# Second mixer of a three-block network on one Trainium2 core: the attention branch's upward product and half of the output projection in three passes of split halves

## The reference, cut to what matters

```python
m   = sigmoid(g_ssm) * (y_ssm @ w_ssm_up) + sigmoid(g_attn) * (y_attn @ w_attn_up)   # 512 -> 1024
x   = x + m @ w_out                                                                  # 1024 -> 1024
h   = rmsnorm(x, norm2_g)
q   = h @ peer_wq                                                                    # 1024 -> 2048, next stage
```

## Time and profile before

| | before |
|---|---|
| time, median of 3 runs | 2174.49 us (2173.45 to 2175.11) |
| the profiled execution's own time | 2174.43 us |
| its span on the core | 2172.4 us |
| PE, DVE, ACT, POOL busy | 95%, 71%, 52%, 32% of the span |
| mean granted TensorE clock | 0.985 of full speed |
| attn_up's first matmul to the next stage's first matmul | 1280.89 to 1330.44 us |

### The profile page before, as it was taken

The page is one execution under the profiler, slowest core; times in us unless marked ns, Lnnn a source line. Parts: engine busy times, 40 slices in busy tenths (PEclk is TensorE's granted clock), DMA queues, the critical chain, the costliest instruction groups (busy, mean ns, idle before and its releaser), DMA issues. The chain is left out here.

```text
span 2172.4 us, 33584 instructions
## 1 busy us (share of the span) xinstructions
PE 2070.5 (95%) x11152; PEld 1705.5 (79%) x11152; DVE 1543.8 (71%) x2577; ACT 1132.3 (52%) x1648; POOL 698.1 (32%) x478
## 2 busy tenths in 40 slices
PE   4999999998999999999999999999999999999998
PEld 4876767776877776777776656999999998888887
DVE  4377898886467788888878841499587776555555
ACT  5364767774345377777550323355544444454444
POOL 6621030003757414000030004599867662000000
PEclk8999999999999989999999999999999999999999
DMA  9873889994557658999832333355544445555554
GB/s 395 304 289 143 340 329 348 348 350 175 200 213 286 232 220 317 345 351 346 328 103 97 126 117 119 110 187 184 183 141 140 145 143 185 192 188 190 193 191 148
DMA packets 76631, 485.65 MB, mean 224 GB/s; under 512 B 9472, under 2 KB 9984, under 8 KB 58624
## 3 DMA queue, kind: packets, MB, share of 16 engines
q1 hardware_dynamic: 75824, 482.88, 61.6%
q10 hardware_dynamic: 720, 1.61, 0.2%
HBM read 483.41 MB, written 1.05 MB: 223 GB/s over the span
## 5 line engine op out<-in xcount | busy, mean ns | idle before, releaser
L1249 DVE TENSOR_TENSOR moe_w_lo<-ring,moe_w_hi 128x1024 fp32r<-128x1024 f32 x376 | 456.1, 1251 | 43.8 <-ACT moe_w_hi L1167 31.9
L1167 ACT ACTIVATE moe_w_hi<-ring 128x1024 fp32r<-128x1024 f32 x376 | 387.0, 1059 | 87.3 <-PE bank L1100 48.0
L3187 POOL TENSOR_TENSOR peer_u_lo<-peer_u,peer_u_hi 128x512 fp32r<-128x512 f32 x255 | 328.1, 1298 | 91.0 <-ACT peer_u_hi L3213 87.7
L3125 PE MATMUL bank<-peer_hn_hi,peer_u_hi 128*128 128x256 f32 x1024 | 293.2, 286 | 3.7 <-ACTq L3200 3.5
L3126 PE MATMUL bank<-peer_hn_lo,peer_u_hi 128*128 128x256 f32 x1024 | 285.8, 279 | 0.0
L3127 PE MATMUL bank<-peer_hn_hi,peer_u_lo 128*128 128x256 f32 x1024 | 285.6, 279 | 0.0
L1081 PE MATMUL bank<-moe_w_hi,moe_slots_hi 128*128 128x512 f32 x512 | 210.2, 411 | 8.3 <-DVE moe_w_lo L1249 4.1
L3213 ACT ACTIVATE peer_u_hi<-peer_u 128x512 fp32r<-128x512 f32 x253 | 159.0, 629 | 112.8 <-PE bank L3127 111.2
L1083 PE MATMUL bank<-moe_w_hi,moe_slots_lo 128*128 128x512 f32 x512 | 200.9, 392 | 0.0
L1082 PE MATMUL bank<-moe_w_lo,moe_slots_hi 128*128 128x512 f32 x512 | 200.4, 391 | 0.0
L3125 PEld LDWEIGHTS bank<-peer_hn_hi,peer_u_hi 128*128 128x128 f32 x1024 | 192.7, 188 | 4.4 <-issue 3.7
(11 more groups left out here) (526 smaller groups left out, 4556.6 us busy)
## 6 DMA issues: line engine op xcount, KB each, us to landing
ring<-in_stream SPq DMA_DIRECT2D x135, 2048.0 KB, 8.8
peer_u<-in_peer_u SPq DMA_DIRECT2D x128, 512.0 KB, 3.3
peer_scores<-in_peer_v SPq DMA_DIRECT2D x86, 512.0 KB, 4.3
sb_mod_ring<-in_ada_t SPq DMA_DIRECT2D x64, 512.0 KB, 6.7
peer_u<-in_peer_v SPq DMA_DIRECT2D x42, 512.0 KB, 4.3
ret_mod_ring<-in_ada_t SPq DMA_DIRECT2D x32, 512.0 KB, 4.8
s_bz<-in_b_channel SPq DMA_DIRECT2D x4, 512.0 KB, 6.0
ring<-in_stream SPq DMA_DIRECT2D x2, 1024.0 KB, 5.9
```

Of the source, the lines that this page charges most:

```text
L1167: act.activation(w_hi[:, q, :], K.ring[:, at % RING, q * CHUNK // Q:(q + 1) * CHUNK // Q], ACT.Copy).then_inc(hi_done, 1)
L1249: dve.tensor_tensor(w_lo[:, q, :], K.ring[:, at % RING, q * CHUNK // Q:(q + 1) * CHUNK // Q], w_hi[:, q, :].bitcast(F32), ALU.subtract).th ...
L3125: pe.matmul(out, u_hi[:, b, k2, :], h_hi[:, k, :], start=(k == 0), stop=False)
L3187: pool.tensor_tensor(u_lo[:, b, :, :], u[:, i, KD // 2 * half:KD // 2 * (half + 1), :], u_hi[:, b, :, :].bitcast(F32), ALU.subtract).then_ ...
```

## The change

Nothing is changed in what is computed. The upward product of attention and the second half of the projection's columns are made in three passes of halves; they borrow the buffers `w_hi`, `w_lo`, `x_hi`, `x_lo` of the next stage's products.

- GpSimd makes the four low quarters of `attn_up` after its second mask, then those of w_out2's second chunk, then those of `peer_wq`: 12 instead of 4.
- ACT makes the high quarters of `attn_up` in the first four turns of the attention loop, those of the second `w_out2` chunk when `attn_up` is used up, and those of `peer_wq` as `project_split(1)` frees each quarter (`out_used`). It also makes a high half of the turned mix.
- DVE takes each unit's values in two steps, a copy to the high half, a wait for it, and the remainder, and makes the low half of the turned mix (`mixed_low`).
- PE's order of the projection becomes (0,0), turn_mixed(1), (1,0), (0,1), (1,1).
- The squares are taken in the order in which the halves come, and the second tile's last square and square root stand ahead of the last high quarter of `peer_wq`.

```diff
+    SPLIT = (n_attn, n_out + 1)
+    ring_quarter = lambda n, q: K.ring[:, n % RING, q * CHUNK // Q:(q + 1) * CHUNK // Q]
...
+            def split_lows(n):                                       # GpSimd, after the second mask
+                for q in range(Q):
+                    pool.wait_ge(split_high, Q * SPLIT.index(n) + q + 1)
+                    pool.tensor_tensor(w_lo[:, q, :], ring_quarter(n, q), w_hi[:, q, :].bitcast(F32),
+                                       ALU.subtract).then_inc(split_low, 1)
+            for n in SPLIT:
+                split_lows(n)
             queries.low(pool, queries.n0, True)
...
             def attn_up(tt, dh):
-                upward(n_attn, S.yaT, tt, dh, 4 + 2 * tt + dh).then_inc(K.chunk_used if tt and dh else attn_made, 1)
+                out, cols = K.bank[:, 4 + 2 * tt + dh, :], slice(dh * 512, (dh + 1) * 512)
+                for k in range(4):
+                    if tt == 0 and dh == 0:
+                        pe.wait_ge(split_low, k + 1)
+                    high, low = w_hi[:, k, cols], w_lo[:, k, cols]
+                    pe.matmul(out, x_hi[:, k, own(tt)], high, start=(k == 0), stop=False)
+                    pe.matmul(out, x_hi[:, k, own(tt)], low, start=False, stop=False)
+                    last = pe.matmul(out, x_lo[:, k, own(tt)], high, start=False, stop=(k == 3))
+                last.then_inc(K.chunk_used if tt and dh else attn_made, 1)
...
+            def project_split(tt):                                   # takes the place of project_out(tt, 1)
+                n, out = n_out + 1, K.bank[:, 2 * tt + 1, :]
+                for k in range(KD):
+                    q, cols = k // 2, slice(k % 2 * COLS, (k % 2 + 1) * COLS)
+                    if k % 4 == 0:
+                        pe.wait_ge(mix_low, 2 * tt + k // 4 + 1)
+                    if tt == 0 and k % 2 == 0:
+                        pe.wait_ge(split_low, Q + q + 1)
...
+                    if tt == 1 and k % 2 == 1 and k < KD - 1:
+                        last.then_inc(out_used, 1)
...
             turn_mixed(1)
+            project_out(1, 0)
             project_out(0, 1)
-            project_out(1, 0)
             project_out(1, 1)
...
                 take_turned(n)                                       # ScalarE, attention loop
                 if n < TT:
                     take_gate(8 + n, n_last, 3, ACT.Copy)
+                if n < Q:
+                    split_high_quarter(n_attn, n)
...
+                for half in range(2):
+                    act.activation(x_hi[:, 4 * half:4 * half + 4, own(tt)],
+                                   K.bank[:, 4 + 2 * tt + half, :].rearrange("p (k t) -> p k t", k=4), ACT.Copy).then_inc(mix_high, 1)
+                if tt == 0:
+                    act.wait_ge(K.chunk_used, n_attn + 1)
+                    for q in range(Q):
+                        split_high_quarter(n_out + 1, q)
...
-            queries.high(act, queries.n0, True)
-            square(0)
-            square(1)
+            square(0, 0)
+            square(2, 1)
+            square(1, 2)
             deviation(0)
-            square(2)
-            square(3)
-            deviation(1)
+            for q in range(Q):
+                if q == Q - 1:
+                    square(3, 3)
+                    deviation(1)
+                act.wait_ge(out_used, q + 1)
+                queries.high_quarter(act, queries.n0, q, True)
...
             def take_values(n):                                      # VectorE, attention loop
-                dve.tensor_copy(S.yaT[:, j, own(tt)], K.bank[:, n % 2, 0:P]).then_inc(o_copied, 1)
+                c.do(dve.tensor_copy(x_hi[:, j, own(tt)], K.bank[:, n % 2, 0:P]))
+                dve.tensor_tensor(x_lo[:, j, own(tt)], K.bank[:, n % 2, 0:P], x_hi[:, j, own(tt)].bitcast(F32),
+                                  ALU.subtract).then_inc(o_copied, 1)
...
+            mixed_low(0)                                             # VectorE, end of the stage
             add_out(0)
             half_square(0)
+            mixed_low(1)
+            add_out(2)
+            half_square(1)
             add_out(1)
...
             normed(0)
-            add_out(2)
-            half_square(1)
             add_out(3)
```

More of the change, by code:

```diff
@@ L2134, in second_mixer_stage @@
     own = lambda tt: slice(tt * P, (tt + 1) * P)
+    Q = 4
+    split_high, split_low, out_used, mix_high, mix_low = (
+        s_(s) for s in ("split_high", "split_low", "out_used", "mix_high", "mix_low"))
+    x_hi, x_lo, w_hi, w_lo = queries.x_hi, queries.x_lo, queries.w_hi, queries.w_lo
+    SPLIT = (n_attn, n_out + 1)
+    ring_quarter = lambda n, q: K.ring[:, n % RING, q * CHUNK // Q:(q + 1) * CHUNK // Q]
     with nc.Block() as block:
@@ L2385, in attn_up @@
             def attn_up(tt, dh):
-                if tt == 0 and dh == 0:
-                    wait_chunk(pe, K, n_attn)
                 pe.wait_ge(o_copied, 4 * tt + 4)
@@ L2403, in project_out @@
             def project_out(tt, dh):
+                if dh == 1:
+                    project_split(tt)
+                    return
                 if tt == 0:
-                    wait_chunk(pe, K, n_out + dh)
+                    wait_chunk(pe, K, n_out)
                 pe.wait_ge(m_taken, 2 * tt + 2)
                 pe.wait_ge(l_used if tt else o_copied, len(units))
-                w = K.ring[:, (n_out + dh) % RING, :].rearrange("p (k c) -> p k c", k=KD)
+                w = K.ring[:, n_out % RING, :].rearrange("p (k c) -> p k c", k=KD)
                 for k in range(KD):
-                    last = pe.matmul(K.bank[:, 2 * tt + dh, :], K.hT[:, k, own(tt)], w[:, k, :], start=(k == 0), stop=(k == KD - 1))
+                    last = pe.matmul(K.bank[:, 2 * tt, :], K.hT[:, k, own(tt)], w[:, k, :], start=(k == 0), stop=(k == KD - 1))
                 last.then_inc(K.chunk_used if tt == 1 else out_made, 1)
+            def project_split(tt):
[6 more added lines that the diff above has]
+                        pe.wait_ge(split_low, Q + q + 1)
+                    high, low = w_hi[:, q, cols], w_lo[:, q, cols]
+                    pe.matmul(out, x_hi[:, k, own(tt)], high, start=(k == 0), stop=False)
+                    pe.matmul(out, x_hi[:, k, own(tt)], low, start=False, stop=False)
+                    last = pe.matmul(out, x_lo[:, k, own(tt)], high, start=False, stop=(k == KD - 1))
+                    if tt == 1 and k % 2 == 1 and k < KD - 1:
+                        last.then_inc(out_used, 1)
+                last.then_inc(K.chunk_used if tt == 1 else out_made, 1)
+                if tt == 1:
+                    pe.wait_ge(K.chunk_used, n + 1)
+                    pe.sem_inc(out_used, 1)
             def turn_normed(tt):
@@ L2556, in take_turned, with split_high_quarter @@
                                ACT.Copy).then_inc(pT_ready, 1)
+            def split_high_quarter(n, q):
+                if q == 0:
+                    act.wait_ge(K.landed[n % RING], 16 * (n // RING + 1))
+                act.activation(w_hi[:, q, :], ring_quarter(n, q), ACT.Copy).then_inc(split_high, 1)
             exponentials(0)
@@ L2827, in _, with mixed_low @@
                 dve.tensor_tensor(gates[:, 0, tt, cols], gates[:, 0, tt, cols], gates[:, 1, tt, cols], ALU.add).then_inc(m_ready, 1)
+            def mixed_low(tt):
+                for half in range(2):
+                    ks, i = slice(4 * half, 4 * half + 4), 2 * tt + half
+                    dve.wait_ge(mix_high, i + 1)
+                    dve.tensor_tensor(x_lo[:, ks, own(tt)], K.bank[:, 4 + i, :].rearrange("p (k t) -> p k t", k=4),
+                                      x_hi[:, ks, own(tt)].bitcast(F32), ALU.subtract).then_inc(mix_low, 1)
             def add_out(n):
```

22 lines of the change are left out of this document (12 added, 10 removed).

## The result

| | before | after |
|---|---|---|
| time, median of 7 runs each | 2175.11 us (2173.45 to 2177.35) | 2181.06 us (2178.51 to 2184.85) |
| ratio, after to before | | 1.0027, 95% interval 1.0017 to 1.0037 |
| profiled execution: own time, span | 2174.43, 2172.4 | 2181.06, 2178.9 |
| attention loop: first logits to attn_up's first matmul | 41.82 | 48.02 |
| attn_up's first matmul to the next stage's first | 49.55 | 48.87 |

What follows compares the result with a forecast made beforehand. It took TensorE, busy 95% of the span, as the bound. Loop cost 3.7 us, plus 48.75 from attn_up to the next stage, minus 49.55, gave +2.9 on 2174.43: 2177.3 us, range 2171.5 to 2180.0.

Steps and rivals of the forecast that it cites:

- What PE saves: In `attn_up` and the projection, 32 products fall from 0.86 to 0.68 us each, together 5.7 us.
- The stall at `turn_mixed(1)`: In the projection, PE stands 0.9 us because ACT's copies of `hT` end after the turn is over.
- The hold-up in the loop: In the attention loop, GpSimd's low quarters hold DVE's L2776 and division; one turn 2.3 us late, the loop 3.7 in all.
- I take held: In the attention loop, the 128x2 L2776 waits for GpSimd's running quarter; loop cost 3.7 us, forecast chance 0.46.
- L2776 is not held: Rival, attention loop: only the divisions are held, loop cost 1.65 us, sum +0.85, time 2175.3; chance 0.20.
- The further 0.4 at turn 4: In the attention loop, quarter 3 meets the next L2776, and that turn is late by a further 0.4 us.
- The clock in the loop: Rival: clock falls at the loop's longer waits, +1.9 us, 2179.2; chance 0.17, shared with one more meeting of held operations.
- The end of the stage: Late `peer_wq` quarters and held scalings put L241 at 48.75 us against 49.55; 4.0 of 4.8 gained are given back.
- one for one: After the stage, all that follows hangs on L241 and shifts by as much as L241 does.

Runs made afterwards that it cites:

- e10_filled: The changed kernel plus two filler float32 products on PE ahead of turn 3 and two ahead of turn 7; 2179.36 us, ratio to before 1.0017.
- e6_columns: The changed kernel with the 128x2 negation of the row maxima written as two single-column instructions; 2177.12 us, ratio to before 1.0007.
- e13: The changed kernel with attention's low quarters on DVE before the values, fillers ahead of turn 7, three `peer_wq` low quarters left to the next stage; 2173.24 us, ratio 0.9985.
- e14: The changed kernel with e13's repairs, and five of eight products of project_out(0,0) put ahead of turn_mixed(1); 2171.31 us, ratio to before 0.9977.
- e1: The changed kernel with attention's upward product and values as before, the projection still split; 2177.18 us, ratio to before 1.0005.
- e3: The kernel before plus four unused GpSimd subtractions at the place of attention's low quarters; 2175.64 us, ratio to before 0.9996.
- e4: The kernel before plus four GpSimd memsets, which read nothing, at the place of attention's low quarters; 2175.83 us, ratio to before 1.0001.
- e12: The changed kernel with attention's product and values as before, and three `peer_wq` low quarters left to the next stage; 2174.58 us, ratio to before 0.9992.
- e17: The kernel before with the negation of the row maxima written as two single-column instructions; 2175.10 us, ratio to before 0.9993.
- e2: The changed kernel with the whole projection as before, attention's upward product still split; 2179.43 us, ratio to before 1.0014.
- e5: The kernel before with the values taken in two steps, nothing else; 2179.60 us, ratio to before 1.0016.
- e7: The changed kernel with three of `peer_wq`'s four low quarters left to the next stage's GpSimd list; 2178.30 us, ratio to before 1.0014.
- e16: The changed kernel with the negation as two single columns and three `peer_wq` low quarters left to the next stage; 2172.16 us, ratio to before 0.9982.
- e8: The changed kernel with attention's low quarters on DVE behind the values, and three `peer_wq` low quarters left to the next stage; 2177.75 us, ratio to before 1.0007.
- e9: The changed kernel with attention's low quarters computed on DVE behind the values of units 4 to 7, not on GpSimd; 2181.14 us, ratio to before 1.0028.

## Why the prediction was wrong

The forecast was 2177.3, within 0.2% of before; it came out at 2181.06, slower by 0.27% and outside the range. Step by step:

**What PE saves, 5.7 us: right.** Passes of `project_split` start 0.227 apart and the last starts at 1323.68, 38.35 behind `attn_up`'s first matmul; its output is added at 38.77, 0.4 later than the sum from 38.15 had it. About 0.1 of that is the clock, still low in `attn_up`'s first matmuls (0.94 over 1285 to 1290): in e10_filled, with the clock at 1.00, the addition comes at 38.65. The rest builds up over the calls (in e10_filled turn_mixed(0) starts at 8.30, 0.15 late). The stall at `turn_mixed(1)` is 0.74; 0.9 was forecast.

**The hold-up in the loop: right, in place and in size.** On the clock of before (1.76 us added), the negation starts at 1258.49 (forecast 1258.5), the division ends at 1262.66 (1262.9), and turn 3 comes at 1262.71 (1262.95). The step "I take held" for 128x2 is shown by the row of 1.61 us and by e6_columns; the rival "L2776 is not held" falls. The prediction's reason for it, more than one column, is too wide: the maximum and the reciprocal write two columns and pass (e6_columns), and what waited with one input is the scalar operation. The Trainium skill, page "VectorE: DVE Perf Modes", section "What auto-detection actually checks", put the even width with the held ones, and the two-column and single-column rows of the negation now agree. The further 0.4 at turn 4 was about 0.1: with the fillers the lag is 2.44 at turn 3 (23.66 against 21.22) and 2.58 at turn 4 (28.76 against 26.18). The loop without the clock's part costs 3.2 us; 3.7 were forecast. One row is cited amiss: L2836 at 1324.04 has an idle GpSimd beside it; the one at 1310.31, beside the low quarters, takes 0.69 as well, so the statement stands.

**The clock in the loop: this step failed.** The sum went by a clock of 1.00, for which I cited the windows 1275 to 1281 of before, with a fall priced at 1.9 us and given 0.17. It fell in both places that the rival named, and the fillers put the two together at 3.0 us, where the rival was priced for one: with both, the sum would have been 2180.3, beyond the 2180.0 of the range. What I had read as a margin was none. TensorE's pause ahead of the last turn and the clock behind it, in the 17 profiled executions:

| pause ahead of the last turn | kernels | clock behind it |
|---|---|---|
| 0.39 us (fillers) | e10, e13, e14 | 1.00 in all 3 |
| 1.78 us | before, e1, e3, e4, e12, e17 | 1.00 in all 6 |
| 2.10 to 2.11 us | after, e2, e5, e7, e16, e6 | 0.50 in 5, 1.00 in e6 |
| 3.24 us | e8, e9 | 0.50 in both |

Ahead of turn 3 the pause is 1.93 to 1.95 us in three kernels (after, e2, e7), and the clock behind it falls to 0.50 in all three; in the others it is 0.55 us or less, and the clock stays at 1.00. There it is the held negation that makes the pause, since it is gone in e6_columns.

At the last turn the 0.33 us of the two-step taking is what carries the pause from 1.78 to 2.10. The step therefore cost not three times 0.33 but, at this one place, over 1 us more; e5_two_step has it alone. Why e6 kept its clock where five others with its pause did not stays open.

**The end of the stage: right.** The first quarter starts 37.47 behind `attn_up`'s first matmul (37.1 forecast), the second tile's scalings end at 46.03 (45.9), GpSimd's last quarter at 48.25 (48.2), the next stage starts at 48.87 (48.75). That the quarters are the bound is shown by the runs without three of them, 4.0 us (e8_both), 3.8 us (e13_repaired) and 3.9 us shorter (e12_plain_later against e1_attn_plain).

**From L241 on, "one for one": not quite.** Behind the start of the next stage the clock is low for 6 us, before for some 4:

```profile
1336.00:1338.00 2.00, 2.00 (x12) 2.00 (x11) 0.00 (x0) 0.00 (x0) 0.00 (x0) 0.50 0.00 0
1338.00:1340.00 2.00, 2.00 (x11) 2.00 (x11) 0.00 (x0) 0.24 (x1) 0.00 (x0) 0.50 0.03 8
```

That is 1 us more. Another low stretch 60 us further on is in 15 of the 17 profiled executions and absent in those of before and of e17_before_columns. How much of either is the change's stays open: e14_around has 6 us of low clock there behind the shortest tail (43.90), e6_columns less than 4 behind a tail as long as that of the changed kernel. The start of the next stage is 5.5 us late, the median 5.9, and the rest is within what executions differ by.

In sum: 3.2 (forecast 3.7) + 3.0 of clock (0) - 0.7 (-0.8) = 5.5, against 2.9.

## What to carry to other kernels

Before work is given to an idle GpSimd, list the VectorE instructions of the critical path that it can hold. Here these were operations with two inputs in SBUF and scalar operations over two or more columns from SBUF to SBUF; a maximum and a reciprocal that write two columns were not held. See whether a small one can be written so that it isn't: one negation as two single columns gave back 5.0 us of the loop in one kernel and 3.7 in another, where the clock fell once. When a change lengthens a pause of TensorE, compare it with the pauses behind which the trace shows the clock held, and where it is longer than all of them, put the fall of the clock into the forecast and not among the rivals. Follow the last instruction of every engine to the stage's barrier in the new order, and leave to the next stage what it can do itself.

## What the runs showed of the hardware

- A GpSimd memset (128x2752, 2.435 us, no input) held a 128x2 negation on VectorE for 1.91 us and let a 128x256 division with two inputs pass in 0.43 us. A GpSimd subtraction of two tensors held both, 1.01 and 2.01 us.
- Two 128x1 negations together took 0.21 us beside a running GpSimd subtraction; the 128x2 one took 1.61. A 128x2 reciprocal (0.15) and a reduction of 128x512 to 128x2 (0.69) passed beside it (e6_columns).
- The same low quarter takes GpSimd 2.35 to 2.38 us and VectorE 1.22 us.
- Two kernels with the same pause of 2.11 us ahead of the last turn went on at 1.00 (e6_columns) and at 0.50 (e16_columns_later). These are single executions, and what else decides it stays open.
